# Two experts of 64 rows in plain fp32 inside a grouped mixture-of-experts stage, and their neighbours' loads re-ordered

## The reference

```
logits = h @ rw + rb
top_v, top_i = top_k(logits, 2)
gates = sum(one_hot(top_i, 8) * softmax(top_v)[..., None], axis=1)
out = 0
for e in range(8):
    out += gates[:, e:e+1] * ((silu(h @ wg[e]) * (h @ wu[e])) @ wd[e])     # 1024 -> 1408 -> 1024
```

## Time and profile before

| | us |
|---|---|
| median of three runs | 1870.2 |
| the profiled execution | 1873.41 |
| its span | 1871.8 |
| PE busy in the span | 1795.5 |
| DVE busy | 1036.4 |
| ACT busy | 796.8 |
| mean granted TensorE clock | 0.974 |
| DMA | 361.77 MB, mean 193 GB/s |

### The profile page before, as it was taken

The page is one execution under the profiler, slowest core; times in us unless marked ns, Lnnn a source line. Parts: engine busy times, 40 slices in busy tenths (PEclk is TensorE's granted clock), DMA queues, the critical chain, the costliest instruction groups (busy, mean ns, idle before and its releaser), DMA issues.

```text
span 1871.8 us, 34051 instructions
## 1 busy us (share of the span) xinstructions
PE 1795.5 (96%) x13659; PEld 1625.3 (87%) x13659; DVE 1036.4 (55%) x1513; ACT 796.8 (43%) x1221; POOL 118.3 (6%) x164
## 2 busy tenths in 40 slices
PE   6999999999999999999999999996999999999998
PEld 4888999998998999989888999995878978968866
DVE  4267461655222223334566633746768867868867
ACT  3346523433222122223366515323556556557554
POOL 1000000001100100000000010003000000000020
PEclk8999999999999999998999999997999999999899
DMA  9932233444776672222422235207769679679576
GB/s 374 370 116 91 86 134 123 162 165 158 273 248 212 231 246 84 97 84 80 147 92 81 100 131 194 90 24 269 285 230 366 214 242 356 228 267 356 195 285 244
DMA packets 96520, 361.77 MB, mean 193 GB/s; under 512 B 12181, under 2 KB 12213, under 8 KB 94577
## 3 DMA queue, kind: packets, MB, share of 16 engines
q1 hardware_dynamic: 65952, 241.07, 36.2%
q0 software_dynamic: 30416, 118.57, 17.6%
HBM read 309.75 MB, written 49.84 MB: 192 GB/s over the span
## 4 chain that ended last, share of the span: by engine, by line
PE 81%; DMA 7%; DVE 5%; issue 3%; ACT 3%; SPq 1%; POOL 0%; POOLq 0%; DVEq 0%; ACTq 0%
PE ps L702 47%; PE ps L830 10%; PE ps L914 8%; PE ps L913 3%; PE ps L860 3%; PE ps L976 2%; DMA g<-gates 2%; DMA xs<-slots 2%; DMA more<-weights 1%; DMA first_ada<-weights 1%; DMA slots<-Yo_large 1%; SPq L503 1%; PE ps L1214 1%; ACT scb L1654 1%; PE ps L1092 1%
## 5 line engine op out<-in xcount | busy, mean ns | idle before, releaser
L702 PE MATMUL ps<-Hh,wh 128*128 128x260 f32 x2080 | 604.1, 290 | 9.4 <-ACT qrt L1683 5.3
L702 PE MATMUL ps<-Hl,wh 128*128 128x260 f32 x2080 | 592.2, 285 | 0.0
L702 PE MATMUL ps<-Hh,wl 128*128 128x260 f32 x2080 | 591.5, 284 | 0.0
L702 PEld LDWEIGHTS ps<-Hh,wh 128*128 128x128 f32 x2080 | 396.6, 191 | 29.8 <-issue 29.0
L702 PEld LDWEIGHTS ps<-Hl,wh 128*128 128x128 f32 x2080 | 396.5, 191 | 0.2
L702 PEld LDWEIGHTS ps<-Hh,wl 128*128 128x128 f32 x2080 | 396.6, 191 | 0.0
L1836 DVE TENSOR_TENSOR wl<-raw,wh 128x1024 fp32r<-128x1024 f32 x168 | 205.5, 1223 | 339.3 <-ACT wh L1439 339.0
L1439 ACT ACTIVATE wh<-raw 128x1024 fp32r<-128x1024 f32 x168 | 177.1, 1054 | 218.0 <-PE ps L702 214.6
L1973 DVE TENSOR_TENSOR wl<-more,wh 128x1024 fp32r<-128x1024 f32 x96 | 114.9, 1221 | 26.6 <-ACT wh L1466 26.2
L1973 DVE TENSOR_TENSOR further<-more,further 128x1024 fp32r<-128x1024 f32 x96 | 114.3, 1220 | 25.0 <-ACT further L1466 24.9
L914 PE MATMUL ps<-XE,wh 128*128 128x512 f32 (+3 forms) x384 | 118.7, 375 | 4.6 <-DVE wl L1973 2.3
(11 more groups left out here) (455 smaller groups left out, 3072.8 us busy)
## 6 DMA issues: line engine op xcount, KB each, us to landing
raw<-weights SPq DMA_DIRECT2D x243, 512.0 KB, 4.2
more<-weights SPq DMA_DIRECT2D x192, 512.0 KB, 5.5
ada<-weights POOLq DMA_DIRECT2D x16, 1536.0 KB, 8.1
slots<-nothing POOLq DMA_DIRECT2D x28, 704.0 KB, 13.0
first_ada<-weights POOLq DMA_DIRECT2D x8, 2048.0 KB, 12.6
gates<-stage POOLq DMA_DIRECT2D x32, 260.0 KB, 2.6
first_ada<-weights SPq DMA_DIRECT2D x16, 512.0 KB, 15.3
g<-gates POOLq DMA_DIRECT2D x2, 3120.0 KB, 12.5
```

The costliest lines, as they stand in the source:

```text
L702: mm = pe.matmul(out, w, v[:, cols], start=first and q == 0, stop=last and q == 2)
```

## The change

**Order and room.** Ranks 6 and 7 become the small experts of pairs 1 and 2, with room for 64 rows; rank 5 moves to pair 3, with 128. Four DVE instructions re-number the ranks before `eids`, and four set the new room before `sweeps` (one old one goes).

**`narrow`**, a new function on PE, ACT and DVE, takes the place of `small` in pairs 1 and 2. Rows and weights stay plain fp32; there is no split. TensorE reads the ring slot itself. Its products have 64 rows held still, and two of them write to the lower and upper half of the partitions. DVE waits for each slab's use and increments `slab_read` (the new name of `slab_low`) by a memset of one element; that frees the ring slot. At its end ACT and DVE split the first three slabs of the next large expert. The preceding `large` leaves its last three look-ahead splits out, and the rows' low part.

**Rows.** POOL now loads the next large expert's rows right after the small rows were turned (`next_loaded`), ahead of the wait for `Yo[0]` and its store.

**The last matrix** is made in pair 2's `narrow`, in pieces after slabs 1, 4, 6, 8, 9, 13, 17 and 18; TensorE turns it after slab 20.

In the diff, cut to its core, `narrow` stands three times: on TensorE, on ACT and on DVE, in this order.

```diff
+FEW = P // 2
+        XP = at("XP", [P, KT, FEW], F32, H0 + 16384)
+        hep = at("hep", [P, FE, FEW], F32, Z0)
+        Yo_few = at("Yo_few", [P, D // 2], F32, H0 + 24576)
-        last_of = at("last_of", [P, NB + 1, P], F32, G0 + 4096)
+        last_of = at("last_of", [P, NB + 1, P], F32, Z0 + 11264)
...
+            def rows_loaded(i):
                 pool.wait_ge(sem("xt_done"), i * 6 + 4)
                 pool.dma_start(xs[:, 0:1, :], slot_rows(i * PAIR_ROWS + CAPS[0], 1)).then_inc(sem("xs_in"), 16)
-                if final:
-                    pool.wait_ge(sem("xt_done"), i * 6 + 6)
+                pool.wait_ge(sem("xt_done"), i * 6 + 6)
+            def next_loaded(i):
+                pool.dma_start(xs[:], slot_rows(i * PAIR_ROWS + PAIR_ROWS, 2)).then_inc(sem("xs_in"), 16)
+            def large_kept(i, more):
                 pool.wait_ge(sem("Yo_made"), i * 3 + 3)
                 pool.dma_start(slot_rows(i * PAIR_ROWS, 2), Yo[0][:]).then_inc(sem("Yo_out"), 16)
...
+            for r in range(1, RANKS - 1):
+                with pool.Fori(full + r, full + (r + 1)) as i:
+                    rows_loaded(i)
+                    next_loaded(i)
+                    large_kept(i, 16 * (r - 1))
+                    pool.wait_ge(sem("Yo_made"), i * 3 + 4)
+                    for q in range(2):
+                        pool.dma_start(half_rows((i + 1) * PAIR_ROWS - CAPS[1], q), Yo_few[FEW * q:FEW * q + FEW, :]).then_inc(sem("Yo_out"), 16)
...
+                def narrow(i, r):
+                    pe.wait_ge(sem("XEh_made"), i * 6 + 6)
+                    if r == RANKS - 2:
+                        pe.matmul(ps[:, 1, 0:P], ones, MSK, start=True, stop=True).then_inc(sem("pe_tail"), 1)
+                    def slab(k):
+                        pe.wait_ge(more_full[k % RING], landed(i, EXP_SLABS + k))
+                        return ring(k % RING)
...
+                    for c in range(CHUNKS):
+                        tiles = chunk_blocks(c)
+                        kks = 1024 // (tiles * 2 * P)
...
+                        for k in range(4 * c, chunk_end(c) + 1):
+                            w = slab(k).rearrange("p (b a j n) -> p b a j n", b=kks, a=2, j=tiles)
+                            for b in range(kks):
+                                kk = (k - 4 * c) * kks + b
+                                for j in range(tiles):
+                                    mm = pe.matmul(ps[FEW * j:FEW * j + FEW, 2 * (c % 2), 0:2 * P].rearrange("p (a n) -> p a n", a=2),
+                                                   XP[:, kk, :], w[:, b, :, j, :], start=kk == 0, stop=kk == KT - 1)
+                            mm.then_inc(sem("slab_used"), 1)
+                            if k % 4 == 1 and 5 <= k:
+                                hidden_turned((k - 5) // 4)
+                            if k in (10, 12, 14, 16):
+                                next_features(i, (k - 10) // 2)
+                            if k == 20 and r == RANKS - 2:
+                                pe.wait_ge(*dve_tail("last_of_made"))
...
+                    for k in range(FE):
...
+                        w = slab(2 * FE + k)
+                        for q in range(2):
+                            mm = pe.matmul(ps[FEW * q:FEW * q + FEW, 4, :], hep[:, k, :], w[:, q * 512:q * 512 + 512],
+                                           start=k == 0, stop=k == FE - 1)
+                        mm.then_inc(sem("slab_used"), 1)
...
+                def narrow(i, r):
...
+                    hidden_kept(CHUNKS - 1)
+                    for k in range(AHEAD):
+                        slab_high(i, PAIR_SLABS + k)
+                    act.wait_ge(sem("slab_used"), i * PAIR_SLABS + (SPLITS + PAIR_SLABS))
+                    act.activation(Yo_few[:], ps[:, 4, :], ACT.Copy).then_inc(sem("Yo_made"), 1)
...
+                def narrow(i, r):
...
+                    for k in range(EXP_SLABS):
+                        dve.wait_ge(sem("slab_used"), i * PAIR_SLABS + (SPLITS + EXP_SLABS + k + 1))
+                        dve.memset(let_go[0:1, r - 1, k:k + 1], 0.0).then_inc(sem("slab_read"), 1)
+                        for c in range(CHUNKS):
+                            if k == chunk_end(c):
+                                multiplied(c)
+                        if k in (10, 12, 14, 16):
+                            features_low(i * 6 + 6, 0, (k - 10) // 2)
+                        if r == RANKS - 2:
+                            if k == 1:
+                                others_marked()
...
+                            if k in (8, 9, 13, 17, 18):
+                                last_matched((8, 9, 13, 17, 18).index(k))
+                    for k in range(AHEAD):
+                        slab_low(i, PAIR_SLABS + k, EXP_SLABS * r)
...
                     for k in range(EXP_SLABS):
-                        slab_low(i, k + AHEAD)
+                        if not few(r) or k + AHEAD < EXP_SLABS:
+                            slab_low(i, k + AHEAD, EXP_SLABS * narrow_ahead(r))
...
-                        if final and k == 4:
-                            last_rows()
...
-                for r in range(1, RANKS):
+                for r in range(1, RANKS - 1):
                     large(full + r, r)
-                    small(full + r, r == RANKS - 1)
+                    narrow(full + r, r)
+                large(full + (RANKS - 1), RANKS - 1)
+                small(full + (RANKS - 1), RANKS - 1)
...
+                dve.tensor_scalar(cnt[4][:], cnt[2][:], float(RANKS), None, ALU.is_gt)
+                link(dve.tensor_scalar(cnt[5][:], cnt[2][:], float(RANKS + 1), None, ALU.is_equal))
+                link(dve.tensor_tensor(cnt[4][:], cnt[2][:], cnt[4][:], ALU.subtract))
+                link(dve.scalar_tensor_tensor(out=cnt[2][:], in0=cnt[5][:], scalar=float(RANKS - 1), in1=cnt[4][:], op0=ALU.mult, op1=ALU.add))
...
+                dve.tensor_scalar(cnt[7][:], cnt[2][:], float(RANKS), float(FEW - CAPS[1]), ALU.is_gt, ALU.mult)
+                dve.tensor_scalar(cnt[8][:], cnt[2][:], E - 1.5, float(CAPS[1] - FEW), ALU.is_gt, ALU.mult)
                 link(dve.tensor_scalar(cnt[4][:], cnt[4][:], float(CAPS[1]), None, ALU.max))
+                link(dve.tensor_tensor(cnt[4][:], cnt[4][:], cnt[7][:], ALU.add))
+                link(dve.tensor_tensor(cnt[4][:], cnt[4][:], cnt[8][:], ALU.add))
...
-                dve.tensor_scalar(sweeps[:, 2:3], posv[8][:, 0, 0:1], float(RANKS), None, ALU.mult)
```

More of the change, by code:

```diff
@@ L431, in added_place, with narrow_ahead, finished, few @@
             return 6 * (m // 4) + m % 4 + 1
-        def finished(name, i, half):
+        def narrow_ahead(r):
+            return max(0, r - 1)
+        def finished(name, i, half, r=0):
             large, small = STEPS_OF[name]
-            return i * (large + small) + half * large
+            return i * (large + small) + (half * large - (small * narrow_ahead(r) if name == "hel_made" else 0))
+        def few(r):
+            return 0 < r < RANKS - 1
+        def half_rows(first, q):
+            return slots[bass.ds(first, FEW), q * (D // 2):(q + 1) * (D // 2)]
+        def landed(i, k):
+            return i * 96 + 16 * (k // EXP_SLABS * 3 + k % EXP_SLABS // RING + 2)
         def ring(f):
@@ L672, in _ @@
                 pool.wait_ge(sem("Yo_out"), i * 32 + 32)
-            with pool.Fori(last, last + 1) as i:
-                small_rows(i, True)
+            for r in range(1, RANKS - 1):
+                with pool.Fori(full + r, full + (r + 1)) as i:
+                    rows_loaded(i)
+                    next_loaded(i)
+                    large_kept(i, 16 * (r - 1))
+                    pool.wait_ge(sem("Yo_made"), i * 3 + 4)
+                    for q in range(2):
+                        pool.dma_start(half_rows((i + 1) * PAIR_ROWS - CAPS[1], q), Yo_few[FEW * q:FEW * q + FEW, :]).then_inc(sem("Yo_out"), 16)
+                    pool.wait_ge(sem("Yo_out"), i * 32 + (32 + 16 * r))
+            with pool.Fori(full + (RANKS - 1), full + RANKS) as i:
+                rows_loaded(i)
+                large_kept(i, 16 * (RANKS - 2))
             for n in range(NB + 1):
@@ L837, in small @@
+                def small(i, r=0):
+                    final = r == RANKS - 1
                     X = XE[1]
@@ L1979, in experts, with others_marked @@
                     features_low(0, 0, r)
-                def last_rows():
+                def others_marked():
                     link(dve.tensor_tensor(flat(row_all), flat(rowf), flat(posv[7]), ALU.add))
@@ L1995, in last_rows @@
                     link(dve.tensor_tensor(at_last[:], at_both[:, 0, :], at_both[:, 1, :], ALU.add))
-                    dve.wait_ge(*pe_tail("slot_ids"))
-                    for n in range(NB + 1):
-                        rows = block_rows(n)
-                        link(dve.tensor_scalar(last_of[0:rows, n, :], ps[0:rows, 6, 0:P], at_last[0:rows, n:n + 1], None, ALU.is_equal))
```

(15 more changed lines are left out.)

146 lines of the change are left out of this document (94 added, 52 removed).

## The result

The changed kernel takes 1843.0 us (median of four runs, 1841.39 to 1847.17) against 1870.0 us for the kernel before beside it: a ratio of 0.9866, 95% interval 0.985 to 0.9881. That is 27 us less; the forecast was 37.7 less. Measured again in six runs it took 1838.9 us, ratio 0.9844 (0.9821 to 0.9867). The profiled execution took 1843.87 us with 1842.3 in its span, 29.5 less than the span of before.

A forecast was written before the change was run, and what follows sets the result against it. TensorE, busy for 96% of the span, was taken as the bound. The terms -15.3 - 13.3 - 1.9 - 8.5 + 1.3 = -37.7 us take the median from 1870.2 to 1832.5, stated as 1833; range 1821 to 1855 us.

The forecast's parts named there:

- TensorE's side of the narrow experts: In each narrow expert: products 30.1 us plus turns 5.0, so TensorE alone would need 35 us.
- waits for slab DMAs from about slab 15 on: Sign expected in the narrow experts' trace: TensorE waits for slab loads from about slab 15.
- The DMA's side: In each narrow expert: last slab lands at 34.5 us, DMA sets the stage, 39 us each; -15.3 and -13.3 us.
- The gap and the clock behind it: At each narrow expert's end: some 2.5 us gap in TensorE's stream, plus 0.9 us for the lower clock.
- Slot freeing by DVE: In the narrow experts: DVE frees each slot after its use; costed at nothing, at most 5.5 us if uncovered.
- Rows loaded earlier: In small 0: TensorE's wait for the next rows goes, -1.9 us; in pairs 1 and 2 already inside the 39 us.
- The last matrix: In large 3: without the matrix block the stall and lower clock go, -8.5 us (bounds -9.5 and 0).
- Router: Before the first expert's rows: eight DVE instructions more and one less, +1.3 us (bounds 1 and 2).
- A: Rival: the clock falls to 1.2 GHz throughout `narrow`, stage 65 us, in all 1884.5 us; chance 0.07.
- B: Rival: large 3 keeps its stall, or each narrow expert takes 44 us; 1842 to 1843, both 1852; chance 0.17.
- C: Rival: the DMA is never late, narrow experts of 35 us, in all 1825 us; chance 0.12.
- D: Rival: an expert exceeds its room, all pairs swept again, over 550 us; chance 0.02 together with anything else.

The follow-up runs named there:

- e7_one_half: Changed kernel, but both products of a pair in the narrow experts write to the same 64 partitions; 1885.8 us, ratio 1.0089.
- e3: Changed kernel, but TensorE leaves out every second gate and up product in the narrow experts; 1838.0 us, ratio 0.9824.
- e8: Changed kernel, with the large result of pairs 1 and 2 stored a second time, to an unread table; 1841.6 us, ratio 0.9852.
- e10: Changed kernel, with the large result of pairs 1 and 2 stored four times, three to an unread table; 1857.4 us, ratio 0.9939.
- e2: Changed kernel, but only the left half of each slab of the two narrow experts is loaded; 1833.0 us, ratio 0.9798.
- e4: Changed kernel, with the large result of pairs 1 and 2 stored only after the narrow expert; 1833.4 us, ratio 0.9801.
- e1_rows_late: Changed kernel, with the next large expert's rows loaded behind the store of the large result again; 1860.8 us, ratio 0.9949.

## Why the prediction was right, and what it missed

The mechanism that the sum rests on held: TensorE's stream became shorter, the DMA took over the narrow experts, and the stall of large 3 went. The 1843 us lie in the range, and none of the signs of being wrong came. The size was 8.2 us short in the profiled execution (37.7 forecast, 29.5 found): 3.2 in the stretch before the router, which is no effect of the change; 3.7 at narrow 1 and 3.1 at narrow 2, each with the clock behind it; and -1.8 of small terms. In the repetition the stages fall short by the same amounts, and the stretch before the router is 2.7 us shorter than before, by chance as well.

**TensorE's side of the narrow experts** (30.1 + 5.0 = 35 us): 35.8 us busy where the DMA is not late. A pair costs 0.44 us for 0.43, and `e7_one_half` shows the parallel halves that the row stood for. The sign "waits for slab DMAs from about slab 15 on" failed: the first wait in narrow 1 is for the 29th slab. By the forecast's own terms slab 15 lands at 5.0 + 4 x 1.28 + 2.6 = 12.7 us, and TensorE, with 35 us for 33 slabs, is not there before 16.

**The DMA's side** was the mis-sized term. That it sets the stage was right (`e3`, `e8`, `e10`). The first load is issued 1.5 us in and lands at 5.4, close to the 1.5 and 5.0 written. But I let the first slab of the next large expert land at 35.8 us, and it landed at 38.2. The bytes say why: up to that moment 366 GB/s over 38.2 us, 14.0 MB, had been moved, where the store and the 23 slabs up to this one are 13.1. The missing 0.9 MB, 2.2 us at 410 GB/s, are parts of later slabs. I had worked it as a line in which slab after slab lands whole. In fact up to 11 loads are under way at once; the time from issue to landing is 11.3 to 11.8 us in narrow 1 where it was 5.5 in the median.

```profile
1530.50:1568.70 38.20, 36.93 (x243) 17.91 (x242) 7.37 (x44) 6.68 (x18) 0.73 (x1) 1.00 0.94 366
```
The next rows are of the DMA issues (count, size, median us to landing):

```profile
more<-weights SPq DMA_DIRECT2D x24, 512.0 KB, 11.8
raw<-weights SPq DMA_DIRECT2D x9, 512.0 KB, 11.3
```

The traces bear this out. In narrow 1 slab 12 lands 3.8 us after slab 11 and slab 13 another 2.6 us later; from slab 14 on they land 1.28 us apart, with one interval of 2.2. So the spread is paid mainly once, where the queue fills. And 0.7 to 0.9 MB too much had been moved at that landing in all twelve narrow stages of six kernels, with no, one, two or four stores. No experiment changed the number of loads under way, so the cause is read from these numbers and not tested. My 2.6 us for the store was good: 2.4 measured per megabyte.

The limit of about 358 GB/s that the Trainium skill has (DMA: Bandwidth & Descriptors, the table at its head, where it is a stack's 716 GB/s divided by two cores) did not bind this lone core. In the second half of narrow 1 it moves 404 to 414 in every window of 2 us, so the measurement stands; 368 over the whole stage is the start from a full ring, not a limit.

**The gap and the clock behind it.** Forecast 2.5 us and 0.9 us of clock each. The gap was 2.54. The lower clock behind it cost 1.5 us each (82.1 to 83.6, 77.2 to 78.7), and it came behind nine of the twelve gaps of this length, so my half price was too low. Behind the gaps of 1.43 us it never came.

**Slot freeing by DVE** at nothing: right for the ring (no slab of the first 28 is waited for). But the memsets had a price where I had not looked: they stand in front of the next large expert's first split. That is hidden behind the DMA in the changed kernel, and it is what is left of the gap in `e2` and `e4`.

**Rows loaded earlier**: -2.1 for the -1.9 of small 0. In the narrow experts the prediction called the saving "already inside the 39 us" and gave no price; `e1_rows_late`, which takes it out, has them 10.8 and 10.5 us longer. It is the term on which the 39 us hang most.

**The last matrix**: 85.7 to 77.2 is -8.5, the number forecast; the lower clock at its beginning takes 1.5 back. **Router**: +0.7 to +1.0 for +1.3. From the first count to the row numbers it takes 15.46 us for 14.31:

```profile
1271.92 0.17 DVE L2017 SCALAR_TENSOR_TENSOR cnt<-ps,cs 128x8 f32<-128x8 f32 x1
...
1287.38 0.17 DVE L2073 TENSOR_TENSOR rowi<-rowf,posv 128x10 int32<-128x10 f32 x1
```

**The rivals.** A, half clock in `narrow`: not once; the granted clock is 1.00 over all of both. The reason given against it held: TensorE was busy for 91 and 93% of the two stages, and its first wait for a slab is 0.28 us long at 1562. The Trainium skill's rule (TensorE: Matmul & The Clock Gate, "HAM oscillation") likewise had no case here, since the bursts are longer than the waits, and the trace agrees. B, 1842 to 1843 or 1852: its lower number is the first measurement, and the forecast's 1833 is not, but the mechanism was not B's. Large 3 kept no stall. Counted as the forecast counts, with the clock behind them, the narrow experts took 42.4 and 41.7 us (40.6 + 1.8, 40.2 + 1.5): at the upper end of its 37 to 42 and more than half of the way to B's 44. But the DMA was not slower than its best, with 404 GB/s and more once the queue was full; it had more bytes to move before the slab that counts. C, the DMA never late: not in this kernel; `e4_late_store`, with 37.2 and 38.1 us, comes near it. D: no second sweep.

**A version better than the change** came out of this: the large result of pairs 1 and 2 stored behind the narrow expert instead of at its head, 1832.1 to 1833.4 us in two measurements, against 1838.9 and 1843.0 for the change. In the rounds measured side by side that is 6.8 us.

## What to carry to other kernels

When TensorE's work in a stage is cut below the DMA's, as here, every byte that runs in the stage is on the path at full price (2.4 us for a megabyte): look for what can be stored or loaded in the neighbouring stages where the DMA has room, before anything else is tuned. When a queue of many equal loads is outstanding, reckon the landing of the next one with parts of the later ones in front of it (0.7 to 0.9 MB here), not by its place in the line alone. A load that hardly matters in one kernel can carry the next: price it in the kernel as it will be. And judge a variant that moves 2 us by its own stages: the stretch before the stage alone scattered by 6 us here.

## What the hardware showed that I had not expected

- A store of 1 MB takes 10.35 us from issue to end beside a full queue of slab loads, and some 5.07 us in the kernel before, where that queue was not as full. It lengthens the narrow stage by only 2.4 us.
- A gap of 1.42 to 1.43 us in TensorE's work left the granted clock at 1.00 nine times out of nine; one of 2.51 to 2.55 us brought 3.4 us at the 1.2 GHz level nine times out of twelve, beginning between the end of the gap (once 0.3 us before it) and 1.7 us later.
- fp32 products with 64 rows held still and 256 columns streamed take 0.44 us a pair when they go to alternate halves of the partitions, and 0.87 when both go to the same half.
- With up to 11 loads of 512 KB under way, a load took 11.3 to 11.8 us from issue to landing, and landings still came 1.28 us apart.
